# Mixer of the second block: five 2 MB weight chunks loaded as two halves each

## The reference, cut to what matters

```python
proj = h @ w_in[l]                      # 2048 -> q 1024, k 256, v 256, u 1024
bu = einsum('lbgh,gph->lbgp', u, b_bar) # drive of a diagonal complex state space model
_, states = lax.associative_scan(_ssm_combine, (a, bu), axis=0)
y = real(einsum('lbgp,ghp->lbgh', states, c_c)) + d * u
out = gelu(y) * sigmoid(gelu(y) @ w_glu + b_glu)
```

## Time and profile before

| what | value |
|---|---|
| median of 3 runs | 3089.47 us (3088.95 to 3092.02) |
| profiled execution, its own time | 3089.37 us |
| its span | 3087.6 us |
| PE busy | 3066.5 us, 99% of the span |
| DVE, ACT, POOL busy | 1846.4, 1453.3, 718.9 us |
| DMA | 598 MB, mean 194 GB/s |

### The profile page before, as it was taken

How to read it: one execution, slowest core, us unless ns; L and a number is a source line. 1 busy time by engine, 2 the same in 40 slices (tenths; PEclk the granted TensorE clock), 3 DMA queues, 4 the chain that set the end, 5 groups by cost and what they waited for, 6 DMA issues and landing times.

```text
span 3087.6 us, 46008 instructions
## 1 busy us (share of the span) xinstructions
PE 3066.5 (99%) x16688; PEld 2623.5 (85%) x16688; DVE 1846.4 (60%) x2369; ACT 1453.3 (47%) x2250; POOL 718.9 (23%) x748
## 2 busy tenths in 40 slices
PE   8999999999999999999999999999999999999999
PEld 7888888888888888888888888888888888888887
DVE  5676655565555567675655555558786555555554
ACT  5454544444344545554343444452565434444343
POOL 1422232141411133041414141125130101001010
PEclk9999999999999999999999999999999999999999
DMA  6534555555656553455556555658534555555554
GB/s 243 191 142 168 191 211 201 203 203 183 218 186 220 202 191 137 164 193 204 203 183 218 189 218 191 225 214 304 189 110 164 191 191 191 191 191 190 191 191 163
DMA packets 70866, 598.06 MB, mean 194 GB/s; under 512 B 14448, under 2 KB 29040, under 8 KB 36672
## 3 DMA queue, kind: packets, MB, share of 16 engines
q1 hardware_dynamic: 59136, 588.17, 52.4%
q10 hardware_dynamic: 11184, 5.48, 0.6%
q0 software_dynamic: 400, 2.44, 0.2%
HBM read 577.92 MB, written 18.15 MB: 193 GB/s over the span
## 4 chain that ended last, share of the span: by engine, by line
PE 95%; DVE 2%; DMA 1%; ACT 1%; issue 0%; ACTq 0%; DVEq 0%
PE bank L680 94%; PE bank L792 1%; DVE w_lo L1732 1%; DMA yrow<-ys 1%; DMA urow<-us 0%; PE bank L951 0%; DMA u<-urow 0%; PE bank L840 0%; DMA par<-params 0%; DVE act_lo L2172 0%; DVE gbuf L2216 0%; DVE sb L2251 0%; PE bank L1118 0%; ACT act_hi L1568 0%; DVE ks L2194 0%
## 5 line engine op out<-in xcount | busy, mean ns | idle before, releaser
L680 PE MATMUL bank<-xg,w_hi 128*128 128x512 f32 (+1 forms) x4256 | 1431.4, 384 | 1.7 <-issue 1.3
L680 PE MATMUL bank<-xg,w_lo 128*128 128x256 f32 (+1 forms) x4064 | 1141.3, 281 | 0.0
L680 PEld LDWEIGHTS bank<-xg,w_hi 128*128 128x128 f32 x4256 | 787.0, 188 | 168.9 <-issue 2.0
L1726 DVE TENSOR_TENSOR w_lo<-raw,w_hi 128x1024 fp32r<-128x1024 f32 x512 | 673.6, 1352 | 426.9 <-ACT w_hi L1233 426.6
L1233 ACT ACTIVATE w_hi<-raw 128x1024 fp32r<-128x1024 f32 x512 | 514.1, 1052 | 634.5 <-PE bank L680 634.3
L680 PEld LDWEIGHTS bank<-xg,w_lo 128*128 128x128 f32 x4064 | 763.7, 188 | 0.9
L680 PE MATMUL bank<-w_hi,act_hi 128*128 128x512 f32 x1920 | 752.8, 392 | 2.0 <-issue 2.0
L680 PE MATMUL bank<-w_hi,act_lo 128*128 128x512 f32 x1920 | 747.7, 389 | 0.0
L680 PE MATMUL bank<-w_lo,act_hi 128*128 128x512 f32 x1920 | 747.3, 389 | 0.0
L1732 DVE TENSOR_TENSOR w_lo<-raw,w_hi 128x1024 fp32r<-128x1024 f32 x510 | 628.4, 1239 | 167.2 <-ACT w_hi L1222 166.6
L1222 ACT ACTIVATE w_hi<-raw 128x1024 fp32r<-128x1024 f32 x514 | 514.4, 1052 | 153.1 <-PE bank L680 123.1
(11 more groups left out here) (346 smaller groups left out, 1956.8 us busy)
## 6 DMA issues: line engine op xcount, KB each, us to landing
raw<-stream SPq DMA_DIRECT2D x260, 2048.0 KB, 7.7
stabs<-ssm_tabs SPq DMA_DIRECT2D x8, 920.0 KB
rdo<-stabs SPq DMA_DIRECT2D x8, 768.0 KB, 6.0
ssm_bc<-smat SPq DMA_DIRECT2D x8, 640.0 KB, 7.2
raw<-stream SPq DMA_DIRECT2D x4, 1024.0 KB, 8.4
stabs<-ssm_f SPq DMA_DIRECT2D x8, 512.0 KB
drv<-stabs SPq DMA_DIRECT2D x8, 512.0 KB, 7.2
trig<-stabs SPq DMA_DIRECT2D x8, 408.0 KB, 4.9
```

What stands on the lines that cost most here:

```text
L680: return pe.matmul(o, a, b, start=start, stop=stop, skip_group_check=True)
L1726: dve.tensor_tensor(flat_lo[j][:, 1024 * h:1024 * h + 1024], flat_raw[r][:, 2048 * j + 1024 * h:2048 * j + 1024 * h + 1024], flat_hi[j][:, ...
```

## The change

The chunks 3 to 7 of the mixer (the fourth to the eighth) are loaded by two DMAs of 1 MB, first k rows 0 to 7 and then 8 to 15. The first half of chunk 3 stays where the chunk was; each of SP's steps 3 to 11 ends with one half, the second half of chunk 3, then both of chunk 4, and so on. The second half counts up the semaphore that the whole chunk did; the first counts up `half_landed`, for which ACT now waits as well ahead of the first tile of such a chunk. ACT still waits for both halves before its first activation.

```diff
-        CHUNKS_BEHIND = {4: 4, 6: 5, 8: 6, 10: 7}
+        HALF_CHUNKS = range(3, 8)
...
+            def half_chunk(c, h):
+
+                if h == 0:
+                    sp.wait_ge(lo_ready, 4 * (R2 + c - 2) + 12)
+                sp.dma_start(raw[c % 2][:, 8 * h:8 * h + 8, :], stream[B2 + c][:, 2048 * h:2048 * h + 2048].rearrange("p (k n) -> p k n", n=CW))\
+                    .then_inc(landed[c % 2] if h else half_landed, 16)
+
             sp.wait_ge(bu_done, 1)
             load_drive(2)
-            chunk(3)
+            half_chunk(3, 0)
             for s in range(3, 12):
...
-                if s in CHUNKS_BEHIND:
-                    chunk(CHUNKS_BEHIND[s])
+                half_chunk(s // 2 + 2, s % 2)
...
             def split_after(T):
 
                 c = (T + 2 - T_B2) // 2
+                if c in HALF_CHUNKS and T % 2 == 0:
+                    act.wait_ge(half_landed, 16 * (DEPTH + c - HALF_CHUNKS[0] + 1))
```

## The result

The changed kernel takes 3101.36 us (median of 7 runs, 3100.06 to 3102.53), the kernel before 3090.72 us in the same comparison (7 runs, 3088.95 to 3092.02). The ratio is 1.0035 with an interval of 1.0024 to 1.0046: 10.6 us slower, between 7.4 and 14.2. The prediction said 3101.0.

The account below looks back on a forecast made before the run. PE, 99% busy, was taken to bound the kernel, with the states made just in time. 3089.4 us plus 9.9 for the later `read_out(6)` plus 1.7 for the lower clock gave 3101.0; range 3088 to 3108.

Parts of the forecast that it names:

- The mechanism: Mixer: states of part n, second half, split, products and scan, states of part n+2 form a closed ring; slower, chance 0.62.
- The length of the ring: Mixer, states of part 0 to part 6: three turns of two slots each, 21.6, 23.6 and 22.9, together 68.1 us.
- Landing of the halves: Ring link from issue of a second half until it is in: 5.8, 7.3 and 7.3 us.
- the upper bound of 8.8: Longest landing allowed for a second half behind `trig` and `rdo`: whole chunk's 11.4 us less 2.6 for 1 MB.
- POOL: Ring link in which POOL makes a part's states: 7.2 us for parts 2, 4 and 6, lower bound 4.5.
- ACT to the scan: Ring links from ACT's split to the end of DVE's scan: 1.1 + 7.0 us, without `x` (0.7) in slot 8.
- `read_out(6)` and the lower clock: PE starts `read_out(6)` 9.9 us later, after a stop of about 6 us; the lower clock behind it adds 1.7 us.
- The splits: ACT's splits of tiles 6, 8 and 10 come near 2115, 2138 and 2161, each released by a half's landing.
- The first stop probably does go: Mixer: PE's first wait for `u` ahead of a drive, 1.96 us, disappears as smaller DMAs let ACT's through.
- the third rival: Mixer: `feed(s)` behind ACT's wait stores `u` late, so drives stop PE too: 3110.5 us, chance 0.10.
- its own list of signs: Wrong if splits come within 2 us of old times, half landings are near 4 us, or PE's stops stay at drives.
- the 7.2 us: Most that could be won in the mixer: 5.5 us of PE waits ahead of drives plus 1.7 of lower clock.

Follow-up runs that it names:

- e3: Changed kernel with each second half issued ahead of the wait for the states and the `trig`, instead of behind the `rdo`: 3091.0 us, ratio 0.9999.
- e1: Changed kernel with chunks 3 to 7 whole again, each issued where its second half stood, at the end of the odd step: 3108.9 us, ratio 1.0057.
- e2: Kernel before with chunks 3 to 7 halved, both halves issued one behind the other at the whole chunk's old place: 3091.4 us, ratio 1.0000.
- e5: Changed kernel with both halves together at the old places, except chunk 5's second half, which waits for the end of step 7: 3095.3 us, ratio 1.0017.
- e8: Changed kernel with the second half issued behind the `trig` but ahead of the `rdo` in steps 5 to 9: 3099.0 us, ratio 1.0027.
- e6: Kernel before with all its whole chunks of the loop moved ahead of the `trig` wait in the same even steps: 3095.5 us, ratio 1.0014.
- e9: Kernel before with only whole chunk 4 moved ahead of the `trig` wait of step 4: 3098.7 us, ratio 1.0016.
- e7: Changed kernel with second halves ahead of the `trig` wait and ACT splitting each half once it is in: 3091.4 us, ratio 1.0002.

## Why the prediction was right, point by point

**The mechanism: right.** The second halves closed a ring over SP, ACT, DVE and POOL. The chain of the changed kernel runs through it link by link for two turns, e3 opens it with one swap and takes the loss away, e1 closes it without halving and loses more, e2 halves without closing it and loses nothing, e5 closes one turn and loses about half.

**The length of the ring: right in sum, with two terms off that cancel.** 68.1 us were worked out, 68.6 measured. The single turns were to be 21.6, 23.6 and 22.9; they were 19.9, 25.6 and 23.1.

- Landing of the halves: taken 5.8, 7.3, 7.3; measured 7.1, 10.0, 8.4. That is 5.1 us too little in all. The second is above the upper bound of 8.8. The rate of 390 GB/s was from a stretch filled by SP's large loads; while the halves were on their way it was less:

```profile
2110.00:2117.00 7.00, 7.00 (x94) 6.93 (x92) 2.30 (x5) 0.00 (x0) 4.45 (x6) 1.00 0.84 303
2130.00:2141.00 11.00, 10.40 (x128) 10.11 (x128) 6.72 (x12) 1.27 (x3) 4.46 (x6) 0.84 0.90 298
```

- POOL: taken 7.2 us for each of parts 2, 4 and 6. Measured 4.5 (2125.13 to 2129.64), 6.9 (2148.36 to 2155.27) and 6.7 (2171.76 to 2178.42). In the first turn DVE did not go on to the odd tile: ACT was waiting for its store of `us`, 8.9 us, because `feed(4)` had been issued late behind the split. Together 3.5 us too much. The trace of before had 6.8 and 7.0 us for parts 4 and 6; the 7.2 of part 2 was taken for all three.
- ACT to the scan: 8.1 taken. In the first turn, from ACT's split at 2117.34 to the end of DVE's scan at 2125.06, 7.7 us; in the second 7.7, in the third (2164.63 to about 2171.7) 7.1 without `x`, where 7.4 was taken. 1.1 us too much in all.

5.1 - 3.5 - 1.1 is the 0.5 us by which the sum was missed. The bounds were wide enough to hold the sum, but not the landing. The mechanism is not luck; that 68.1 met 68.6, and so 3101.0 the 3101.4, is.

**`read_out(6)` and the lower clock: right.** 9.9 us forecast, 10.5 found; 1.7 forecast behind the stop, 1.3 found. The stop was 3.6 us and not about 6, because PE was late already by its stops at drives and at `ys`. The clock fell three times in this part of the kernel, after the stops of 2.71, 3.53 and 3.59 us, where it fell once before; the first two lie ahead of `read_out(6)`, and only the third adds to its delay. A granted clock of 0.83 shows in that stretch:

```profile
2172.00:2182.00 10.00, 6.41 (x76) 6.09 (x75) 9.93 (x14) 2.72 (x4) 8.17 (x8) 0.83 0.95 348
```

9.93 of 10 us for DVE: at the end of the ring DVE too has no reserve.

**The splits: right in kind, each a little late.** Near 2115, 2138 and 2161 were named, 1.2 us to be added for the other execution; found 2117.3, 2140.6 and 2164.6, so 1.1, 1.4 and 2.4 us behind that, each released by the landing of a half. The `trig` issues were to be 2108, 2130 and 2154 and were 2109.8, 2129.7 and 2155.3.

**What was said of the drives: wrong.** "The first stop probably does go": it shrank from 1.96 to 0.59 us, but others grew, and the sum rose from 5.5 to 7.8 us. `feed` behind the blocked ACT, which I had kept for the third rival, did take part. PE was to stop ahead of `read_out(2)`, `read_out(4)` and `read_out(6)`; it stopped ahead of the last alone, and ahead of the others at the drives of the same slots, for 2.71 and 3.53 us, waiting for `u`. Behind these drives the states were no stop any more: part 2 was ready at 2129.64, before the drive started at 2130.34, and part 4 at 2155.27, while the drive of 2154.39 still ran. By its own list of signs ("or if PE's stops stay at the drives") this part of the prediction was wrong. Nor did the halves let ACT's small DMAs through: the loads of `u` issued 1.4 and 2.2 us behind a half took 9.8 and 10.2 us. So in slots 6 and 8 two delays with one origin, ACT held up by the landing, ran side by side, and only the end of the ring, `read_out(6)`, is set by the states.

**The reading of the page: one slip.** The prediction says that all waits of PE for a DMA come to 5.5 us in three pieces. That is the line for `u` alone; the waits of PE in the kernel before also have this, in the first third of the kernel:

```profile
PE bank L792 <- DMA x<-xrow: 6.4, 1, 6.4
```

The sum does not use it, since the three pieces are all that there is in the mixer; but the 7.2 us are what could be won there and not in the kernel.

**The rule of the Trainium skill on a DMA's length** (DMA: Bandwidth & Descriptors, Anatomy of one DMA: a fixed part of about 2 us plus bytes at 436 GB/s) would by the prediction's estimate have made the time 3098.6. The landings of the second halves, 5.9 to 10.0 us for 1 MB in the changed kernel and e8 with others in the queue, don't agree with 4.4 us; the measured ones decide. The page gives its fit for DMAs that GpSimd issues, which the prediction does not say; these are SP's. What it says against halving, a fixed part paid twice, did not show: e2 is at 1.0000.

**The Trainium skill's rule on turns among queues** (DMA: Bandwidth & Descriptors, Queues, rings and completion order) let one expect that a small DMA of ACT is little held up by SP's large ones. No run isolates it. Loads of 136 KB took 10.9 and 10.4 us behind a chunk in e6 and e9, and 5.8 us without one in the kernel before, so the time of a small load does depend on its company. What the prediction drew from it, that halving brings ACT's small DMAs little, agrees with the runs: e3 and e7, halved with the ring open, are at 0.9999 and 1.0002.

## What to carry to other kernels

When a load is moved in an in-order queue, write down for each wait that it is now behind what produces that semaphore, and follow it back: if the producer needs the load itself, a few steps later, the move has closed a ring, and its length over its number of slots is the new pace. A 2 us reserve in landing is no reserve for a step that takes 10 us. Halving these transfers cost nothing measurable; where each half stands made the whole difference, and the half that a consumer waits for should be issued ahead of waits for that consumer's results. Issuing earlier is not always better: e6 and e9 moved whole chunks forward, closed no ring and still lost 4 to 7 us; the waits that show there are for small loads of `u`, the longest issued behind a chunk.

## What the runs showed of the hardware that I had not expected

- The second halves, 1 MB each, took 5.9 to 10.0 us from issue to landing in the changed kernel and e8, with 0.4 to 1.2 MB issued just ahead of them; 2 MB at the same place took 10.0 to 10.3 us in e1, hardly more than the slowest half.
- POOL's product of 128x272 takes 0.77 us while DVE stands and up to 1.76 us while DVE subtracts `w_lo`: 4.5 us for the six operations of a part in one case, 6.7 to 7.2 in the other. DVE is slower for it too: its two subtractions take 2.36 us while POOL stands (2118.43 in the changed kernel) and 3.19 us beside its products (2103.22). Timeline of POOL after, an operation of part 0 (DVE busy) and one of part 1 (DVE waiting):

```profile
2103.58 1.75 POOL L2620 TENSOR_TENSOR pprod<-trig,zi 128x272 f32<-128x272 f32 x1
...
2112.60 0.77 POOL L2620 TENSOR_TENSOR pprod<-trig,zi 128x272 f32<-128x272 f32 x1
```

- The length of a stop alone does not decide the clock behind it. PE came back at the lower clock after stops of 2.71, 3.53 and 3.59 us in the changed kernel, 2.40 in the kernel before and 3.75, 4.62 and 4.72 in e1, and after one of only 2.15 us in e8. After 2.99 us at `ys` in e5 it stayed at the higher one (read-out matmuls of 0.32 to 0.34 us), as after 2.58 us in e6 (a drive of 1.17 us). After 3.61 us in e5 it fell 0.6 us behind the restart: the line below, against 0.34 us for the first read-out matmuls behind that stop.

```profile
2171.38 0.50 PE L690 MATMUL bank<-wi,rdo 128*64 128x67 f32 x4
```
